# A two-layer hybrid encoder trunk: level masks made early on GpSimd, one product and one bank moved, and a stage's second chunk split between the halves of u

## The chip, the cores and the metric

The kernel runs as one program on one core of a Trainium2 chip. The core has TensorE (PE in the rows; PEld is its weight load), VectorE (DVE), ScalarE (ACT), GpSimd (POOL) and SyncE (SP), which run side by side and meet only at semaphores. The metric is the device time of one execution in microseconds (us), lower is better.

## The reference, cut to what matters

The input x is 512 tokens by 1024 channels, float32. Each of two layers does three residual stages:

```
x = x + 0.5 * rms_norm(swiglu(rms_norm(x), w_in, w_out))            # FFN, 2816 wide
u = rms_norm(x);  parts = u @ mix_w_in                              # mixer, 4872 wide
y_a = gated_delta_rule(conv+silu(q,k,v), beta, decay)  -> rms_norm * silu(z)
y_b = sliding_window_attention(rope(q), rope(k), v, sinks)
x = x + rms_norm((sig(gate_a) * (y_a @ w_a) + sig(gate_b) * (y_b @ w_b)) @ mix_w_out)
x = x + 0.5 * rms_norm(swiglu(...))                                 # second FFN
```

The delta rule works in chunks of 64 tokens. For each of 8 chunks and 4 heads it needs the inverse of a unit triangular 64x64 matrix A = I + lower(k_beta k^T * decay), the masked products q k^T * decay, and a state that is carried from chunk to chunk.

## The kernel before, in words

**Weights.** All weights come as one stream of chunks of 128x1024 float32. For each chunk SyncE loads `raw` (two slots), ScalarE rounds it to `whi` (L906, or L1243 for the first four chunks), and VectorE makes the remainder `wlo = raw - whi` (L1285). These two steps are called the split of a chunk. Both halves have a ring of four slots. SyncE may load chunk c+3 only when the split of chunk c+1 is done, since the slot of `raw` is free then. TensorE multiplies hi by hi, hi by lo and lo by hi (L520 to L522), 24 matmuls of 512 columns for a full chunk.

**Order of work.** Each engine has its own instruction list, written out by hand, and runs it strictly in order. In the mixer the lists come from one table, `mix_steps()`: for chunk j = 3 to 47 of the stage, after chunk j's matmuls (TensorE) or after the split of chunk j+3 (ScalarE, VectorE), each engine goes through the steps of `s[j]` and does its own part of each. A step that needs PSUM names its bank in `banks_of`. A bank goes from step to step in the order of the table: TensorE may fill it (`use`) only when the reader of the step before has given it back.

**The delta rule's inverse.** VectorE solves the 16x16 diagonal blocks by back substitution (step `solve`, s[14], L1539 and L1541, 30 small instructions that each wait for the one before). The blocks go out to DRAM and come back (SyncE, j = 16 and 17), and step `zb` (s[17]) spreads them to Z and its transpose Zt. Two levels (4 and 5) then join blocks of 16 to 32 and of 32 to 64. For each level and each half i of the 16 matrices: GpSimd multiplies the matrix by the level's mask into `Cs` (`level_mask`, L1738), TensorE multiplies Cs by Zt (`invp`, L719), ScalarE copies the result to `Pm` (L1122), which GpSimd has zeroed before (L1777), TensorE multiplies Pm by Z (`invd`, L731), and VectorE subtracts from Z and Zt (L1559). Level 4's masks are made by step `cmask` in s[14]. `Cs` and `Pm` exist once, so level 5's masks and zeroes are made in step `invp` of s[21], behind level 4's matmuls.

**Other steps of the change.** `vtr` transposes v (TensorE, then four ScalarE copies, L1116). `qtr` transposes q, and ScalarE squares it out of bank 5 (L1106) and gives the bank back (L1110). `qk` makes q k^T for 128 tokens (L705), and VectorE multiplies it into `attnT` (L1519). `sc` makes the attention scores in bank 5 (L783), VectorE finds their maximum (L1592 to L1595) and ScalarE takes the exponential (L1176) and gives the bank back. `evac` is ScalarE's copy of a finished PSUM tile to SBUF (L1050). Chunk 20 may write bank 0 only after `evac` 16 (tile `sk`), which stands in s[19].

**Between stages.** At a hand-over (`boundary`) the next stage's u is made while the last matmuls of the old stage run. u has two halves h of 256 tokens, each of eight pieces k. TensorE transposes the scaled x (`turn_tile`, L532) into the banks. For every k in turn ScalarE writes `uhi` (`u_round`, L956) and VectorE writes `ulo` (`u_rest`, L1327); piece k+2 of uhi waits for piece k of ulo. The first chunk of the new stage is split ahead of half 0, the second (c+1) behind it, then the third and fourth. TensorE's `first_group` begins with half 0: tiles m = 0 and 1 for k = 0 and 1, then tiles m = 2 and 3 for k = 0 and 1, then the second chunk. The transposes of half 0 lie in the same four banks as the tiles:

```
if h == 0 and k == 0:
    pe.wait_ge(u_lo.h, u_lo.at(L, u0 + (3, 4, 7, 8)[m]))
```

So tile 2 may start only when ulo piece 6 is written, and tile 3 when piece 7 is. There are five hand-overs with a next stage, and the same order stands once at the start of the kernel.

Of the kernel before, what the change touches and what calls it, by code (L numbers as in the profile page):

```python
# [79 lines left out]
def mix_steps():  # L80

    s = {j: [] for j in range(M_CHUNKS)}
    s[3] = [("evac", 0), ("evac", 1), ("ba",), ("evac", 2), ("evac", 3), ("conv", 0)]
    s[4] = [("bat",), ("gprep",), ("silu", 0), ("conv", 1)]
    s[5] = [("gsum",), ("conv", 2), ("silu", 1)]
    s[6] = [("conv", 3), ("silu", 2), ("decay", 0), ("decay", 1)]
    s[7] = [("evac", 4), ("evac", 5), ("evac", 6), ("evac", 7), ("silu", 3), ("off", 0), ("off", 1), ("conv", 4)]
    s[8] = [("ktr", 0), ("ktr", 1), ("conv", 5), ("silu", 4)]
    s[9] = [("ktr", 2), ("ktr", 3), ("knorm",), ("conv", 6), ("silu", 5)]
    s[10] = [("conv", 7), ("silu", 6), ("kk", 0), ("kk", 1)]  # L90
    s[11] = [("evac", 8), ("evac", 9), ("evac", 10), ("evac", 11), ("silu", 7), ("kk", 2), ("kk", 3), ("conv", 8)]
    s[12] = [("conv", 9), ("silu", 8)]
    s[13] = [("conv", 10), ("silu", 9)]
    s[14] = [("conv", 11), ("silu", 10), ("solve",), ("cmask",)]
    s[15] = [("evac", 12), ("evac", 13), ("evac", 14), ("evac", 15), ("silu", 11), ("swap", 0), ("swap", 1)]
    s[16] = [("vtr", 0), ("swap", 2), ("rope", 0), ("rope", 1)]
    s[17] = [("vtr", 1), ("swap", 3), ("zb",), ("vtr", 2)]
    s[18] = [("qk", 0), ("qk", 1), ("rope", 2), ("rope", 3)]
    s[19] = [("evac", 16), ("evac", 17), ("swap", 4), ("invp", 0, 4), ("vtr", 3), ("invp", 1, 4), ("rope", 4)]
    s[20] = [("vwin", 0), ("invd", 0, 4), ("qtr", 0), ("kmask",), ("invd", 1, 4)]  # L100
    s[21] = [("invp", 0, 5), ("vwin", 1), ("invp", 1, 5), ("qtr", 1), ("qk", 2), ("amask",)]
    s[22] = [("invd", 0, 5), ("invd", 1, 5), ("sc", 0)]
    s[23] = [("evac", i) for i in range(18, 22)] + [("zcp",), ("vx", 0), ("vx", 1)]
    s[22].insert(1, ("qtr", 2))
    s[23].insert(0, ("qtr", 3))
    s[24] = [("zx", 0), ("zx", 1), ("lq",)]
    s[25] = [("qk", 3)]
    s[26] = []
    for n in range(NCH):
        if n:  # L110
            s[22 + n].append(("sc", n))
        s[23 + n].insert(0, ("scn", n))
        s[24 + n].append(("pt", n))
        s[25 + n].append(("pv", n))
    for t in range(TT):
        if t:
            s[24 + 3 * t].append(("ks", t))
        s[25 + 3 * t].append(("sv", t))
        s[26 + 3 * t].append(("so", t))
        s[27 + 3 * t].append(("on", t))  # L120
        s[28 + 3 * t].insert(0, ("onm", t))
        s[29 + 3 * t].append(("otr", t))
    for i in range(4):
        s[24 + i].append(("zsilu", i))
    for g in range(4):
        s[27 + 4 * g] = [("evac", 22 + 4 * g + i) for i in range(4)] + s[27 + 4 * g]
    s[37] += [("ybs", 0), ("ybs", 1)]
# [13 lines left out]
def banks_of(step):  # L141

    k, x = step[0], (step[1] if len(step) > 1 else 0)
    if k in ("ba", "bat", "gsum", "vwin", "sc", "qtr"):
        return (5,)
    if k == "vtr":
        return ((5, 4, 6, 7)[x],)
# [64 lines left out]
def trunk(nc, wstream, xin, par, gpost, consts, rope, out):  # L212
# [3 lines left out]
    with ctx:  # L216
# [53 lines left out]
        Cs = at("Cs", [P, 16, CH], 52 * kb)  # L270
        Pm = at("Pm", [P, 16, CH], 56 * kb)
        tri = at("tri", [P, SB, SB], 57 * kb)
# [241 lines left out]
        def _(pe):  # L514
# [129 lines left out]
            def mixer(L):  # L644
# [6 lines left out]
                def do(step):  # L651
# [39 lines left out]
                    elif k == "qtr":  # L691
                        t = step[1]
                        use(L, step, 5)
                        pe.wait_ge(silu_done.h, silu_done.at(L, 12))
                        for h in range(H):
                            last = pe.transpose(bank(5, h * P, P), kq[:, 1, h, t * P:(t + 1) * P], ident)
                        done(last, 5)
                    elif k in ("kk", "qk"):
# [8 lines left out]
                    elif k == "invp":  # L707
# [9 lines left out]
                        for c in range(8 * i, 8 * i + 8):  # L717
                            for a in range(2):
                                last = pe.matmul(bank(b, (c % 8) * 32, 32, CH * a, CH * a + CH),  # L719
                                                 half(Cs, a, c), block_cols(half(Zt, a, c), lev, 0), start=True, stop=True)  # L720
                        done(last, b)
                    elif k == "invd":
                        i, lev = step[1], step[2]
                        got(("invp", i, lev), banks_of(("invp", i, lev))[0])
                        for n, b in enumerate(banks_of(step)):
# [175 lines left out]
        def _(act):  # L901
# [47 lines left out]

            def u_round(L, st, h):  # L950

                for k in range(KT):
                    act.wait_ge(turned.h, turned.at(L, 8 * (st - 1) + 4 * h + 3 + k // 4))
# [9 lines left out]
            def boundary(L, n, c, unit):  # L963
# [63 lines left out]
            def mixer(L):  # L1027
# [3 lines left out]
                def do(step):  # L1031
# [66 lines left out]
                    elif k == "qtr":  # L1098
                        t = step[1]
                        ready(step, 5)  # L1100
                        if t == 0:
# [3 lines left out]
                        for h in range(H):  # L1105
                            last = act.activation(tmp[:, 4 + t % 2, h * P:(h + 1) * P], bank(5, h * P, P), ACT.Square,  # L1106
                                                  accum_out=ssq[:, 4 * t + h:4 * t + h + 1])
                        last.then_inc(ssq_done.h, 1)
                        act.wait_ge(ssq_done.h, ssq_done.at(L, t + 1))
                        act.sem_inc(misc_out[5].h, 1)  # L1110
                    elif k == "vtr":
# [6 lines left out]
                    elif k == "invp":  # L1118
                        i, lev, b = step[1], step[2], banks_of(step)[0]
                        ready(step, b)  # L1120
                        act.wait_ge(p_zero.h, p_zero.at(L, 2 * (lev - LEVELS[0]) + i + 1))
                        act.activation(block_cols(Pm[:, 8 * i:8 * i + 8, :], lev, 0), half_cols(bank(b, 0, 256), lev),  # L1122
                                       ACT.Copy).then_inc(misc_out[b].h, 1)
# [126 lines left out]
            x_scale(0, 0, 1)  # L1250
            u_round(0, 0, 0)
            first_split(1)
            x_square(0, 0, 2)
            first_split(2)
# [14 lines left out]
        def _(dve):  # L1269
# [51 lines left out]

            def u_rest(L, st, h):

                for k in range(KT):
                    c = slice(2 * P * h, 2 * P * h + 2 * P)
# [4 lines left out]
            def boundary(L, n, c):  # L1330
# [352 lines left out]
            split(0, 0, 0)  # L1683
            u_rest(0, 0, 0)
            split(0, 1, 1)
            x_mean(0, 0, 2)
            split(0, 2, 2)
# [13 lines left out]
        def _(pool):  # L1701
# [32 lines left out]
            def mixer(L):  # L1734
                def level_mask(i, lev):

                    s8 = slice(8 * i, 8 * i + 8)
                    pool.tensor_tensor(Cs[:, s8, :], NN[:, s8, 0:CH], many(con[:, K_LEV + 64 * (lev - LEVELS[0]):][:, 0:64], 8),  # L1738
                                       ALU.mult).then_inc(c_done.h, 1)

                def do(step):
# [17 lines left out]
                    elif k == "cmask":  # L1759
                        pool.wait_ge(silu_done.h, silu_done.at(L, 11))  # L1760
                        for i in range(2):
                            level_mask(i, LEVELS[0])
                    elif k == "invp":
                        i, lev = step[1], step[2]
                        s8 = slice(8 * i, 8 * i + 8)
                        if lev == LEVELS[0]:
                            if i == 0:
                                pool.wait_ge(z1_done.h, z1_done.at(L, 2))
                        else:
                            last = ("invp", i, lev - 1)  # L1770
                            b = banks_of(last)[0]
                            pool.wait_ge(misc[b].h, misc[b].at(L, USE[last, b] + 1))
                            level_mask(i, lev)
                            used = ("invd", i, lev - 1)
                            pool.wait_ge(misc[banks_of(used)[0]].h, misc[banks_of(used)[0]].at(L, USE[used, banks_of(used)[0]] + 1))
                            pool.sem_inc(pool_begun.h, 1)
                        pool.memset(Pm[:, s8, :], 0.0).then_inc(p_zero.h, 1)  # L1777

# [156 lines left out]
```

## Time and profile before

| What | Value |
|---|---|
| Median of 3 runs | 2229.74 us (2229.63 to 2230.46) |
| The profiled execution's own time | 2229.16 us |
| Its span | 2227.4 us |
| TensorE busy | 2199.8 us of the span (99%), 11292 matmuls |
| VectorE, ScalarE, GpSimd busy | 1013.8, 841.5, 74.7 us (46%, 38%, 3%) |
| Mean granted TensorE clock | 0.999 of full speed |

A matmul's record is longer than the time to the next matmul's start, since matmuls are pipelined. Times of TensorE are therefore read from start to start: a 128x256 matmul follows the one before after 0.12 us, a 128x512 one after 0.23 us, and what is over that is a wait or a change of shape.

### The profile page before, as it was taken

The page shows a single profiled execution, that of the slowest core. Times are in us where ns is not written, and L with a number is a line of the kernel's source. Part 1 is how long each engine was busy: PE and PEld are TensorE (multiplying, and loading weights), DVE is VectorE, ACT ScalarE, POOL GpSimd, SP SyncE. Part 2 cuts the span into 40 slices and gives each one's busy share as a digit, 9 for nine tenths or more (in the row PEclk, how much of TensorE's full clock was granted, in tenths as well). Part 3 has the DMA queues.
Part 4 walks back from the last instruction along what each step waited for, and adds up shares of the span by engine and source line. Part 5 has one row for each costly group of instructions (what it writes and reads, how often), then busy time and mean ns, then how long its engine had stood idle before and what let it go on. Part 6 is the DMA issues. An engine that isn't in the chain of part 4 may idle for free. (4 is left out here: it accounts for less than half of the span.)

```text
span 2227.4 us, 28889 instructions
## 1 busy us (share of the span) xinstructions
PE 2199.8 (99%) x11292; PEld 1842.5 (83%) x11292; DVE 1013.8 (46%) x1438; ACT 841.5 (38%) x1491; POOL 74.7 (3%) x104
## 2 busy tenths in 40 slices
PE   7999999999999999999999999999999999999998
PEld 7888888888788888888888888887888888888887
DVE  4434324595536544342253433246954455344323
ACT  5323214656542533231252322156555425333211
POOL 0000000011000100000000000010100001000000
PEclk9999999999999999999999999999999999999999
DMA  4232222332223232223232232223322233322232
GB/s 164 95 101 93 99 95 83 126 84 76 67 76 139 90 111 95 94 94 104 78 113 95 94 104 94 95 76 133 83 68 67 85 142 97 103 95 94 96 102 77
DMA packets 71126, 215.83 MB, mean 97 GB/s; under 512 B 18928, under 2 KB 19440, under 8 KB 70256
## 3 DMA queue, kind: packets, MB, share of 16 engines
q1 hardware_dynamic: 69008, 201.82, 27.3%
q0 software_dynamic: 2016, 12.58, 1.6%
q8 instruction: 72, 1.18, 0.2%
q14 instruction: 30, 0.25, 0.0%
HBM read 206.77 MB, written 7.60 MB: 96 GB/s over the span
## 5 line engine op out<-in xcount | busy, mean ns | idle before, releaser
L1285 DVE TENSOR_TENSOR wlo<-raw,whi 128x1024 fp32r<-128x1024 f32 (+1 forms) x376 | 459.9, 1224 | 892.3 <-ACT whi L906 883.3
L520 PE MATMUL ps<-uhi,whi 128*128 128x512 f32 (+1 forms) x2208 | 826.8, 374 | 5.6 <-DVE ulo L1327 2.0
L522 PE MATMUL ps<-uhi,wlo 128*128 128x512 f32 (+1 forms) x2208 | 818.6, 371 | 0.0
L521 PE MATMUL ps<-ulo,whi 128*128 128x512 f32 (+1 forms) x2208 | 818.6, 371 | 0.0
L906 ACT ACTIVATE whi<-raw 128x1024 fp32r<-128x1024 f32 (+1 forms) x372 | 390.9, 1051 | 930.9 <-PE ps L522 549.0
L520 PEld LDWEIGHTS ps<-uhi,whi 128*128 128x128 f32 x2208 | 416.0, 188 | 80.0 <-issue 6.0
L522 PEld LDWEIGHTS ps<-uhi,wlo 128*128 128x128 f32 x2208 | 415.8, 188 | 71.7
L521 PEld LDWEIGHTS ps<-ulo,whi 128*128 128x128 f32 x2208 | 416.1, 188 | 69.4
L567 PE MATMUL ps<-whi,hhi 128*128 128x512 f32 x704 | 274.4, 390 | 0.0
L569 PE MATMUL ps<-whi,hlo 128*128 128x512 f32 x704 | 274.0, 389 | 0.0
L568 PE MATMUL ps<-wlo,hhi 128*128 128x512 f32 x704 | 273.9, 389 | 0.0
L569 PEld LDWEIGHTS ps<-whi,hlo 128*128 128x128 f32 x704 | 132.1, 188 | 27.7
L568 PEld LDWEIGHTS ps<-wlo,hhi 128*128 128x128 f32 x704 | 132.2, 188 | 27.2
L567 PEld LDWEIGHTS ps<-whi,hhi 128*128 128x128 f32 x704 | 132.2, 188 | 27.1
L993 ACT ACTIVATE tmp<-ps 128x512 f32<-128x512 f32 x88 | 52.8, 599 | 98.9 <-PE ps L522 98.5
L1366 DVE SCALAR_TENSOR_TENSOR tmp<-tmp,ps 128x512 f32<-128x512 f32 x88 | 60.2, 684 | 41.8 <-ACT tmp L993 41.8
L996 ACT ACTIVATE hhi<-tmp 128x512 f32 (+1 forms) x88 | 55.4, 629 | 52.1 <-DVE tmp L1369 52.1
L1710 POOL TENSOR_TENSOR ry<-msy,neghalf 128x1 f32<-128x1 f32 x24 | 17.9, 744 | 1492.9 <-DVE msy L1292 1492.9
L1375 DVE SCALAR_TENSOR_TENSOR hlo<-tmp,hhi 128x512 f32 (+1 forms) x88 | 60.6, 689 | 12.0 <-ACT hhi L996 10.8
L1369 DVE TENSOR_TENSOR tmp<-tmp,ps 128x512 f32<-128x512 f32 x88 | 60.5, 688 | 8.4 <-PE ps L522 1.2
L1469 DVE SCALAR_TENSOR_TENSOR tmp<-cv,prm,tmp 128x512 f32<-128x512 f32 x72 | 54.0, 750 | 8.1 <-ACT tmp L1057 6.4
L1327 DVE SCALAR_TENSOR_TENSOR ulo<-ps,prm,uhi 128x256 fp32r<-128x256 f32 x96 | 42.1, 480 | 28.9 <-ACT uhi L956 28.9
(213 smaller groups left out, 1548.2 us busy)
## 6 DMA issues: line engine op xcount, KB each, us to landing
raw<-in_wstream_dram SPq DMA_DIRECT2D x368, 512.0 KB, 3.4
x_home<-x POOLq DMA_DIRECT2D x4, 1024.0 KB, 4.4
x<-x_home POOLq DMA_DIRECT2D x2, 2048.0 KB, 8.5
gain<-in_gp_dram POOLq DMA_DIRECT2D x6, 512.0 KB, 6.2
x<-in_x_dram SPq DMA_DIRECT2D x4, 512.0 KB, 8.1
raw<-in_wstream_dram SPq DMA_DIRECT2D x8, 256.0 KB, 3.7
out_dram<-x SPq DMA_DIRECT2D x8, 256.0 KB, 2.0
rcs<-in_rope_dram POOLq DMA_DIRECT2D x2, 512.0 KB, 3.7
```

The source lines that it names most:

```text
L520: pe.matmul(o, lh, bhi, start=first, stop=False)
L521: pe.matmul(o, lh, blo, start=False, stop=False)
L522: return pe.matmul(o, ll, bhi, start=False, stop=last)
L567: pe.matmul(o, shi[:, k, tok], whi[:, s, w], start=k == 0, stop=False)
L568: pe.matmul(o, shi[:, k, tok], wlo[:, s, w], start=False, stop=False)
L569: last = pe.matmul(o, slo[:, k, tok], whi[:, s, w], start=False, stop=k == kn - 1)
L906: act.activation(whi[:, s, 0:cols], raw[:, s % RAWS, 0:cols], ACT.Copy).then_inc(hi_done.h, 1)
L996: act.activation(hhi[:, bass.ds(it * 2 + i, 1), :].rearrange("p a s -> p (a s)") if not isinstance(it, int) else hhi[:, 2 * it + i, :], tm ...
L1285: dve.tensor_tensor(wlo[:, s, 0:cols], raw[:, s % RAWS, 0:cols], whi[:, s, 0:cols].bitcast(f32), ALU.subtract) \
L1366: dve.scalar_tensor_tensor(tmp[:, i, :], tmp[:, 4 + i, :], 1.0, bank(4 * odd + 2 * i), ALU.add, ALU.mult).then_inc(tile_read.h, 1)
L1369: dve.tensor_tensor(tmp[:, 2 + i, :], tmp[:, i, :], bank(4 * odd + 2 * i + 1), ALU.mult).then_inc(tile_read.h, 1)
L1375: dve.scalar_tensor_tensor(lo, tmp[:, 2 + i, :], 0.5, hi.bitcast(f32), ALU.mult, ALU.subtract) \
```

## The change

Four edits:

1. In the mixer, `Cs` and `Pm` of level 5 get memory of their own (`Ctop`, `Ptop`; level 4's zeroed buffer becomes `Plow`). Step `cmask` (s[14]) now makes the masks of both levels, four GpSimd multiplications with two memsets between, and step `zb` zeroes level 5's buffer. Step `invp` has no GpSimd part any more.
2. `("vtr", 0)` goes from s[16] to s[19], behind the two evacs; `("qk", 3)` goes from s[25] to the end of s[31].
3. `("qtr", 3)` uses bank 4 instead of bank 5.
4. At every hand-over, and at the start of the kernel, the split of the second chunk goes from behind half 0 of u to between pieces 3 and 4 of it, on ScalarE and on VectorE. TensorE's order is as it was.

```diff
-    s[16] = [("vtr", 0), ("swap", 2), ("rope", 0), ("rope", 1)]
+    s[16] = [("swap", 2), ("rope", 0), ("rope", 1)]
-    s[19] = [("evac", 16), ("evac", 17), ("swap", 4), ("invp", 0, 4), ("vtr", 3), ("invp", 1, 4), ("rope", 4)]
+    s[19] = [("evac", 16), ("evac", 17), ("vtr", 0), ("invp", 0, 4), ("swap", 4), ("vtr", 3), ("invp", 1, 4), ("rope", 4)]
-    s[25] = [("qk", 3)]
+    s[25] = []
+    s[31] += [("qk", 3)]
-    if k in ("ba", "bat", "gsum", "vwin", "sc", "qtr"):
+    if k in ("ba", "bat", "gsum", "vwin", "sc"):
         return (5,)
+    if k == "qtr":
+        return ((5, 5, 5, 4)[x],)
...
-        Pm = at("Pm", [P, 16, CH], 56 * kb)
+        Cl = [Cs, at("Ctop", [P, 16, CH], 72 * kb)]
+        Pl = [at("Plow", [P, 16, CH], 76 * kb), at("Ptop", [P, 16, CH], 56 * kb)]
...
-            def u_round(L, st, h):
-                for k in range(KT):
+            def u_round(L, st, h, ks=range(KT)):
+                for k in ks:
...
-                u_round(L1, st, 0)
+                u_round(L1, st, 0, range(4))
                 next_split(L, c, 1, unit)
+                u_round(L1, st, 0, range(4, KT))
                 y_square(L, n, 3, unit)
...
-                u_rest(L1, st, 0)
+                u_rest(L1, st, 0, range(4))
                 split(L, c + 1, (c + 1) % RING)
+                u_rest(L1, st, 0, range(4, KT))
                 x_add(L, n, 2)
...
                         for i in range(2):
                             level_mask(i, LEVELS[0])
-                    elif k == "invp":
-                        ...
+                        for i in range(2):
+                            pool.memset(Pl[0][:, 8 * i:8 * i + 8, :], 0.0).then_inc(p_zero.h, 1)
+                        for i in range(2):
+                            level_mask(i, TOP)
+                    elif k == "zb":
+                        pool.wait_ge(z1_done.h, z1_done.at(L, 2))
+                        for i in range(2):
+                            pool.memset(Pl[1][:, 8 * i:8 * i + 8, :], 0.0).then_inc(p_zero.h, 1)
```

The start of the kernel has the same reordering around `first_split(1)` and `split(0, 1, 1)`.

## Rows read from the trace of the kernel before

**Rows 1.** The page, part 1: busy us, share of the span, instructions.

```profile
PE 2199.8 (99%) x11292; PEld 1842.5 (83%) x11292; DVE 1013.8 (46%) x1438; ACT 841.5 (38%) x1491; POOL 74.7 (3%) x104
```

**Rows 2.** Waits, whole span: engine, line, waited for: total us, times, longest.

```profile
PE ps L783 <- DVE attnT L1519: 2.6, 2, 1.3
PE ps L520 <- ACT sk L1050: 1.7, 2, 0.8
PE ps L783 <- ACTq L1110: 0.6, 2, 0.3
...
PEld ps L520 <- DVE wlo L1285: 3.2, 6, 0.5
...
PEld ps L532 <- ACT tmp L947: 2.5, 6, 0.5
```

**Rows 3.** Timeline, PE, first hand-over: start us, us, instruction, [idle before].

```profile
383.02 0.34 PE L520 MATMUL ps<-uhi,whi 128*128 128x256 f32 x1
...
384.39 0.28 PE L522 MATMUL ps<-uhi,wlo 128*128 128x256 f32 x1
384.99 0.38 PE L520 MATMUL ps<-uhi,whi 128*128 128x256 f32 x1 [0.32 <-DVE wlo L1285]
```

**Rows 4.** Timeline, ACT, the same hand-over.

```profile
379.69 0.87 ACT L956 ACTIVATE uhi<-ps,prm 128x256 fp32r<-128x256 f32 x2 [0.25 <-DVE ulo L1327]
...
382.63 1.05 ACT L906 ACTIVATE whi<-raw 128x1024 fp32r<-128x1024 f32 x1
```

**Rows 5.** Timeline, DVE, the same hand-over.

```profile
381.29 0.88 DVE L1327 SCALAR_TENSOR_TENSOR ulo<-ps,prm,uhi 128x256 fp32r<-128x256 f32 x2 [0.21 <-ACT uhi L956]
382.37 0.88 DVE L1327 SCALAR_TENSOR_TENSOR ulo<-ps,prm,uhi 128x256 fp32r<-128x256 f32 x2 [0.21 <-ACT uhi L956]
383.71 1.23 DVE L1285 TENSOR_TENSOR wlo<-raw,whi 128x1024 fp32r<-128x1024 f32 x1 [0.46 <-ACT whi L906]
```

**Rows 6.** Timeline, ACT, the fourth chunk's split in that hand-over.

```profile
388.40 1.06 ACT L906 ACTIVATE whi<-raw 128x1024 fp32r<-128x1024 f32 x1 [0.95 <-DMA raw<-in_wstream_dram]
```

**Rows 7.** Timeline, PE, start of the kernel.

```profile
18.50 0.36 PE L520 MATMUL ps<-uhi,whi 128*128 128x256 f32 x1 [0.51 <-DVE ulo L1327]
```

**Rows 8.** Timeline, POOL, layer 0: masks and memsets.

```profile
483.89 2.54 POOL L1738 TENSOR_TENSOR Cs<-NN,con 128x512 f32<-128x512 f32 x2 [26.91 <-DVE kq L1482]
...
512.46 0.53 POOL L1777 MEMSET Pm<- 128x512 f32 x1 [8.36 <-PE ps L731]
```

**Rows 9.** Timeline, DVE, layer 0: the substitution and what follows it.

```profile
483.94 1.29 DVE L1541 TENSOR_TENSOR sol<-sol,prod 128x15 f32<-128x15 f32 x1
485.26 1.22 DVE L1539 TENSOR_TENSOR prod<-tri,sol 128x28 f32<-128x28 f32 x1
486.51 0.19 DVE L1541 TENSOR_TENSOR sol<-sol,prod 128x28 f32<-128x28 f32 x1
...
492.97 0.69 DVE L1285 TENSOR_TENSOR wlo<-raw,whi 128x512 fp32r<-128x512 f32 x1
...
498.67 1.23 DVE L1285 TENSOR_TENSOR wlo<-raw,whi 128x1024 fp32r<-128x1024 f32 x1
...
512.74 0.69 DVE L1587 TENSOR_TENSOR tmp<-tmp 128x512 f32<-128x512 f32 x1
```

**Rows 10.** Timeline, ACT, layer 0, before chunk 20.

```profile
503.39 1.06 ACT L906 ACTIVATE whi<-raw 128x1024 fp32r<-128x1024 f32 x1 [0.30 <-DMA raw<-in_wstream_dram]
504.35 0.58 ACT L1050 ACTIVATE sk<-ps 128x512 f32<-128x512 f32 x1
```

**Rows 11.** Timeline, PE, layer 0: chunk 20 begins.

```profile
505.08 0.47 PE L520 MATMUL ps<-uhi,whi 128*128 128x512 f32 x1 [0.81 <-ACT sk L1050]
```

**Rows 12.** Timeline, PE, layer 0: qk 3, and the scores behind it.

```profile
556.11 1.05 PE L705 MATMUL ps<-kq 128*128 128x128 f32 x8
...
559.67 0.67 PE L783 MATMUL ps<-skz,sq 128*128 128x256 f32 x2 [1.33 <-DVE attnT L1519]
```

**Rows 13.** Timeline, ACT, layer 0: last read of the scores before.

```profile
554.97 0.21 ACT L1176 ACTIVATION_READ_ACCUMULATOR pexp<-ps,mneg 128x1 f32 x1
```

More of the change, by code:

```diff
@@ L691, in do @@
                     elif k == "qtr":
-                        t = step[1]
-                        use(L, step, 5)
+                        t, b = step[1], banks_of(step)[0]
+                        use(L, step, b)
                         pe.wait_ge(silu_done.h, silu_done.at(L, 12))
                         for h in range(H):
-                            last = pe.transpose(bank(5, h * P, P), kq[:, 1, h, t * P:(t + 1) * P], ident)
-                        done(last, 5)
+                            last = pe.transpose(bank(b, h * P, P), kq[:, 1, h, t * P:(t + 1) * P], ident)
+                        done(last, b)
                     elif k in ("kk", "qk"):
@@ L719, in do @@
                                 last = pe.matmul(bank(b, (c % 8) * 32, 32, CH * a, CH * a + CH),
-                                                 half(Cs, a, c), block_cols(half(Zt, a, c), lev, 0), start=True, stop=True)
+                                                 half(Cl[lev - LEVELS[0]], a, c), block_cols(half(Zt, a, c), lev, 0), start=True, stop=True)
                         done(last, b)
@@ L723, in do @@
                         i, lev = step[1], step[2]
+                        Pm = Pl[lev - LEVELS[0]]
                         got(("invp", i, lev), banks_of(("invp", i, lev))[0])
@@ L1098, in do @@
                     elif k == "qtr":
-                        t = step[1]
-                        ready(step, 5)
+                        t, b = step[1], banks_of(step)[0]
+                        ready(step, b)
                         if t == 0:
@@ L1105, in do @@
                         for h in range(H):
-                            last = act.activation(tmp[:, 4 + t % 2, h * P:(h + 1) * P], bank(5, h * P, P), ACT.Square,
+                            last = act.activation(tmp[:, 4 + t % 2, h * P:(h + 1) * P], bank(b, h * P, P), ACT.Square,
                                                   accum_out=ssq[:, 4 * t + h:4 * t + h + 1])
@@ L1109, in do @@
                         act.wait_ge(ssq_done.h, ssq_done.at(L, t + 1))
-                        act.sem_inc(misc_out[5].h, 1)
+                        act.sem_inc(misc_out[b].h, 1)
                     elif k == "vtr":
@@ L1121, in do @@
                         act.wait_ge(p_zero.h, p_zero.at(L, 2 * (lev - LEVELS[0]) + i + 1))
-                        act.activation(block_cols(Pm[:, 8 * i:8 * i + 8, :], lev, 0), half_cols(bank(b, 0, 256), lev),
+                        act.activation(block_cols(Pl[lev - LEVELS[0]][:, 8 * i:8 * i + 8, :], lev, 0), half_cols(bank(b, 0, 256), lev),
                                        ACT.Copy).then_inc(misc_out[b].h, 1)
@@ L1250, in _ @@
             x_scale(0, 0, 1)
-            u_round(0, 0, 0)
+            u_round(0, 0, 0, range(4))
             first_split(1)
+            u_round(0, 0, 0, range(4, KT))
             x_square(0, 0, 2)
@@ L1320, in x_mean, with u_rest @@
                 dve.tensor_scalar(msx[:, t:t + 1], ssx[:, t:t + 1], 1.0 / D, EPS, ALU.mult, ALU.add).then_inc(msx_done.h, 1)
-            def u_rest(L, st, h):
-                for k in range(KT):
+            def u_rest(L, st, h, ks=range(KT)):
+                for k in ks:
                     c = slice(2 * P * h, 2 * P * h + 2 * P)
@@ L1683, in _ @@
             split(0, 0, 0)
-            u_rest(0, 0, 0)
+            u_rest(0, 0, 0, range(4))
             split(0, 1, 1)
+            u_rest(0, 0, 0, range(4, KT))
             x_mean(0, 0, 2)
@@ L1737, in level_mask @@
                     s8 = slice(8 * i, 8 * i + 8)
-                    pool.tensor_tensor(Cs[:, s8, :], NN[:, s8, 0:CH], many(con[:, K_LEV + 64 * (lev - LEVELS[0]):][:, 0:64], 8),
+                    pool.tensor_tensor(Cl[lev - LEVELS[0]][:, s8, :], NN[:, s8, 0:CH], many(con[:, K_LEV + 64 * (lev - LEVELS[0]):][:, 0:64], 8),
                                        ALU.mult).then_inc(c_done.h, 1)
@@ L1762, in do @@
                             level_mask(i, LEVELS[0])
-                    elif k == "invp":
[L1764 to L1777, printed above, removed]
+                        for i in range(2):
[6 more added lines that the diff above has]
+                            pool.memset(Pl[1][:, 8 * i:8 * i + 8, :], 0.0).then_inc(p_zero.h, 1)
                 pool.wait_ge(u_lo.h, u_lo.at(L, 16))
```

## The prediction

> **What bounds the kernel now.** I read the page's busy shares first: TensorE is busy 99% of the span and no other engine half of it [rows 1]. A busy share of 99% leaves 27.6 us (2227.4 - 2199.8) in which TensorE has nothing, and since none of the four edits adds or removes a matmul, only these gaps can move. The second view is the list of waits, cut to TensorE and its weight load [rows 2]. Here the reader is to see how small and how placed the gaps are. The scores (L783) wait twice for qk 3's multiplication on VectorE (1.3 us each), chunk 20 waits twice for the `sk` copy, the scores wait twice for qtr 3's bank, the second chunk of a stage waits six times for `wlo`, and the transposes of a hand-over wait for the scaled x (six times, at most 0.5 each; one is at the start of the kernel, so some 2.0 over the five hand-overs). All that the change aims at is therefore about 10 us. The third view is the timeline of each engine around each of these places, since a fix of 0.5 us is easily paid for with an instruction of 1.2 us in front of something else.
>
> **Edit 4, the second chunk between the pieces of u.** Now TensorE ends the first chunk's half with a matmul at 384.39 and starts the second chunk at 384.99 [rows 3]. At a pitch of 0.12 that is 0.48 too late, and about 0.1 more goes in the restart: 0.6 per place. It waits for the `wlo` of 383.71 + 1.23 = 384.94 [rows 5]. But the same rows show what stood ahead of it: tile 2 started at 383.02, on the very tick at which ulo piece 6 allowed it (the pair of pieces 6 and 7 starts at 382.37). There is no slack on that second wait.
>
> With the new order: uhi pieces 2 and 3 end at 379.69 + 0.87 = 380.56. `whi` takes 1.05 and overlaps the end of the pair ahead a little [rows 4]: it ends near 381.50. `wlo` follows 0.03 later and takes 1.23: 382.76. The four remaining ulo pieces come in two pairs, 1.09 apart (381.29, 382.37) [rows 5]; the first can start at 382.68, the last at 383.77 instead of 382.37, 1.40 later. Tile 2 then starts at about 384.40 instead of 383.02. Twelve matmuls follow before the second chunk, which has its split at 382.76 and waits no more. So 1.38 is lost and 0.6 is won: +0.8 per place. ScalarE could hide its share (its 1.05 us runs while VectorE works), VectorE could not: its split is in series with ulo.
>
> Something comes back later in the hand-over. The split of c+1 ends 2.2 us earlier (382.76 for 384.94), so SyncE's load of the fourth chunk starts 2.2 earlier, and ScalarE's wait of 0.95 for it goes [rows 6]. The scaled x of tokens 384 to 511 stands behind it on ScalarE and comes between 0 and 0.95 earlier, while TensorE arrives 0.8 later. So the wait of at most 0.5 in each of five places [rows 2] goes wholly. At the start of the kernel the third tile already waits 0.51 for ulo [rows 7]; there the same insertion costs the same 0.8 and there is nothing to win back. Sum of edit 4: 6 x 0.8 - 2.0 = +2.8 us. Bounds: if ulo 6 and 7 were not delayed, 6 x -0.6 - 2.0 = -5.6; if nothing comes back, 6 x 0.8 = +4.8, and a full 1.38 at six places without the won 0.6 is +8.3.
>
> **Edit 1, all masks in the substitution.** Level 4's two masks are made there already, 2.54 us for two [rows 8]. Within just these 2.54 us the two VectorE instructions that run take 1.29 and 1.22 us, and the first after them, of the same kind, takes 0.19 [rows 9]. Each has two SBUF inputs and stood still until GpSimd's multiplication was over. The two masks thus cost VectorE (1.29 - 0.19) + (1.22 - 0.19) = 2.1 us. Two more masks in the same chain cost the same again: +2.1 per layer. The masks that go from s[20] and s[21] blocked whole-chunk splits there; nothing on TensorE's side waited for these, so their removal is priced at 0.
>
> The two memsets: a memset at 512.46 to 512.99 overlaps a two-input VectorE instruction at 512.74, which takes its usual 0.69 [rows 8, 9]. I take 0 for them. Upper end: 0.53 each, 1.06 per layer.
>
> The Trainium skill has a rule on this, SBUF — State Buffer, section "Who interferes with whom": a VectorE instruction with two SBUF inputs contends with a GpSimd instruction that reads SBUF and not with one that only writes it, and the later one to issue blocks fully. The page's section "Terms" says more broadly that the shared pair is exclusive for the full instruction, which taken alone would charge the memsets too. By the first the sum is mine, by the second it is the rival with the memsets below. The memset row speaks for the first.
>
> Is the substitution on TensorE's path? VectorE runs without an idle row from the substitution over the split of chunk 18 (492.97) to the split of chunk 20 (498.67, ends 499.90) [rows 9]. That last one lets SyncE load chunk 22, whose `whi` ScalarE starts at 503.39 after waiting for that DMA, then the `sk` copy at 504.35 to 504.93, then chunk 20 at 505.08 with 0.81 idle [rows 9 to 11]. Every link is tight, so all of 2.1 arrives at chunk 20, whatever part of it TensorE has waited for at chunk 18 before. That TensorE has 0.6 us less in s[16] and as much more in s[19] (vtr 0) changes only where it waits: the copy of `sk`, near 507.0, stays the last to come. Net +2.1 per layer. Lower bound 0 (the delay is absorbed in a slack that I do not see), upper 2 x 1.28 + 1.06 = 3.6.
>
> **Edit 2, qk 3 out of s[25].** TensorE's 8 matmuls move, nothing is saved by that. Scores 3 start at 559.67 after 1.33 idle [rows 12]; where the second chunk waited, the start came 0.16 later than the idle says (0.48 against 0.32, rows 3), so 1.5 us are lost here. Bank 5 must wait for qk 3's multiplication, which VectorE reaches late. Without it bank 5 is held by scores 2, whose last read ends at 554.97 + 0.21 = 555.18 [rows 13], while TensorE arrives near 559.67 - 1.5 - 0.9 = 557.3 (0.9 for the eight matmuls that are gone, 1.05 with the last one's tail). Slack 2 us, so no new wait: -1.5 per layer. In s[31] qk 3 costs what it cost, and its reader needs it only in s[35]. Bounds -1.6 and 0.
>
> **Edit 3, qtr 3 in bank 4.** The scores' wait of 0.3 [rows 2] goes. Next late is the copy of tile 18 on ScalarE, which stands behind the same squares and which chunk 24 needs; it leaves about half: -0.15 per layer, bounds -0.4 and 0.
>
> **Sum.** +2.8 + 2 x (2.1 - 1.5 - 0.15) = +3.7 us. Against the profiled execution's own 2229.16 that gives 2232.9; the median of the runs shown is 0.6 above that execution, so the forecast is 2233.5, 0.17% more than before. What a measurement of this kernel can tell from no change is about 0.2%, or 4.5 us: the forecast is a small loss inside that.
>
> **Rivals.**
>
> A, slower: the shared SBUF access charges GpSimd's whole time in the substitution, memsets too, in series with the chain above: 3.6 instead of 2.1 per layer, +3.0, 2236.5. For it: tight chain, and four GpSimd instructions in a row leave no gap. Against it: the memset row. It decides from 2.5 us per layer upwards, where the total passes 4.5.
>
> B, no change: the new masks don't reach TensorE (VectorE's small instructions slip between them, or chunk 20 was late for another reason): -2 x 2.1, 2229.3. Against it: two blocked instructions out of two.
>
> C, faster: the split between the pieces does not delay tiles 2 and 3, because VectorE finishes it while it would idle for uhi. Then edit 4 gives its -5.6 instead of +2.8: 2225.1. For it: VectorE idles 0.21 per pair [rows 5]. Against it: these are 0.42 of the 1.23 that the split takes.
>
> **Chances.** The forecast 0.62, of which about a third lies past 4.5 us, since its own range is 2231.5 to 2235.5; A 0.15; B 0.14; C 0.09. Faster by over 0.2% (below 2225.3): 0.08; slower (above 2234.2): 0.35; within: 0.57. The range takes in B's middle and A's: 2229.3 to 2236.8.
>
> **What would show it.** Right: TensorE's list of waits has `ulo` instead of `wlo` at the six first groups, near 1.2 us each, and no wait of L532 for `tmp`; four VectorE instructions of the substitution are over 1 us instead of two, and chunk 18 waits about 2 us for its split; L783 waits no more for L1519 or L1110; the fourth chunk's `whi` no longer waits for its DMA. Wrong: a first group without a wait for `ulo` (then C), a substitution of 9.1 us as now (483.9 to 493.0, rows 8 and 9; then B), one of over 12.3 us (then A), or scores 3 still idle, for ScalarE's scores 2 or VectorE's softmax.

## The result

Before takes 2229.91 us (median of 9 runs, 2229.14 to 2232.23) and after 2236.55 us (9 runs, 2234.43 to 2238.49). The ratio is 1.0028, with a 95% interval of 1.0019 to 1.0036: the change makes the kernel slower by about 6.6 us, or 0.28%, which is small and clear of the interval. The profiled execution of after took 2236.55 us, with a span of 2234.8; the span before was 2227.4, so 7.4 us are to be found between the two traces.

The page of after, part 1 (busy us, share of the span, instructions), beside [rows 1]:

```profile
PE 2204.0 (99%) x11292; PEld 1846.8 (83%) x11292; DVE 1013.1 (45%) x1438; ACT 840.4 (38%) x1491; POOL 71.8 (3%) x104
```

TensorE executes the same 11292 matmuls, yet it is *busy* for 4.2 us longer (2204.0 against 2199.8). Only 3.2 of the 7.4 us are idle time. A wait makes an engine hardly busier (in [rows 3] the record behind a wait is 0.38 long, the one ahead of it 0.28), so this line already says that something besides the waits has changed.

The list of TensorE's waits of after (engine, line, waited for: total us, times, longest), all of it without its weight load, beside [rows 2]:

```profile
PE ps L536 <- ACT tmp L952: 10.9, 1, 10.9
PE ps L524 <- DVE ulo L1334: 8.1, 7, 1.4
PE ps L524 <- DVE wlo L1292: 4.7, 2, 2.4
PE ps L524 <- ACT sk L1056: 0.6, 1, 0.6
```

The line on `ulo` has this one in its place in the kernel before, both of its waits at the start of the kernel:

```profile
PE ps L520 <- DVE ulo L1327: 2.0, 2, 1.5
```

The first line of after is the start of the kernel. The scores' line (L788 here) is gone from the list, both for `attnT` and for the bank, and so are the scaled-x waits of the five hand-overs. New are five waits of 1.2 for `ulo`, in the place of those for `wlo` at a stage's start, and 2.4 and 2.3 us for `wlo` at chunk 18 of the two layers.

The first hand-over, timeline of TensorE (start us, us, instruction, [idle before]), beside [rows 3]:

```profile
385.22 0.35 PE L524 MATMUL ps<-uhi,whi 128*128 128x256 f32 x1 [1.20 <-DVE ulo L1334]
...
386.72 0.28 PE L524 MATMUL ps<-uhi,whi 128*128 128x256 f32 x1
```

Tile 2 starts 2.20 later than in [rows 3] (385.22 for 383.02), of which 0.82 was there already, from the start of the kernel: 1.38 are new. The second chunk (386.72) has no bracket, so no wait, and is 1.73 later (384.99 before): 0.47 is won back. VectorE and ScalarE in that hand-over, beside [rows 4 to 6]:

```profile
382.37 1.23 DVE L1292 TENSOR_TENSOR wlo<-raw,whi 128x1024 fp32r<-128x1024 f32 x1 [0.46 <-ACT whi L911]
383.51 0.87 DVE L1334 SCALAR_TENSOR_TENSOR ulo<-ps,prm,uhi 128x256 fp32r<-128x256 f32 x2
384.59 0.88 DVE L1334 SCALAR_TENSOR_TENSOR ulo<-ps,prm,uhi 128x256 fp32r<-128x256 f32 x2 [0.21 <-ACT uhi L961]
```

```profile
387.88 1.04 ACT L911 ACTIVATE whi<-raw 128x1024 fp32r<-128x1024 f32 x1
```

The split stands between the two halves of `ulo`, for 1.23 us in series. The fourth chunk's `whi` starts without the 0.95 of waiting for its DMA [rows 6].

The substitution in layer 0, VectorE, beside [rows 9]:

```profile
485.35 1.29 DVE L1549 TENSOR_TENSOR sol<-sol,prod 128x15 f32<-128x15 f32 x1
486.68 1.22 DVE L1547 TENSOR_TENSOR prod<-tri,sol 128x28 f32<-128x28 f32 x1
487.94 0.19 DVE L1549 TENSOR_TENSOR sol<-sol,prod 128x28 f32<-128x28 f32 x1
...
488.87 1.25 DVE L1549 TENSOR_TENSOR sol<-sol,prod 128x48 f32<-128x48 f32 x1
490.16 1.22 DVE L1547 TENSOR_TENSOR prod<-tri,sol 128x55 f32<-128x55 f32 x1
...
496.44 0.69 DVE L1292 TENSOR_TENSOR wlo<-raw,whi 128x512 fp32r<-128x512 f32 x1
```

GpSimd beside it, for [rows 8]:

```profile
485.31 2.55 POOL L1747 TENSOR_TENSOR Cs<-NN,con 128x512 f32<-128x512 f32 x2 [26.95 <-DVE kq L1490]
487.80 0.99 POOL L1773 MEMSET Plow<- 128x512 f32 x2
488.75 2.55 POOL L1747 TENSOR_TENSOR Ctop<-NN,con 128x512 f32<-128x512 f32 x2
```

Four VectorE instructions of over 1.2 us (all four are shown), two within each pair of multiplications; within the memsets (487.80 to 488.79) the one shown takes its usual 0.19. The way from the first blocked instruction to the split of chunk 18 is 11.1 us long (485.35 to 496.44), where it was 9.0 [rows 9].

And what follows on TensorE, with the granted clock. First the timeline at chunk 18 and at 541, then stretches of the span (window: length, busy time and count of PE, PEld, DVE, ACT, POOL; granted clock; DMA share; GB/s):

```profile
497.18 0.79 PE L524 MATMUL ps<-uhi,whi 128*128 128x512 f32 x1 [2.41 <-DVE wlo L1292]
...
540.75 0.63 PE L525 MATMUL ps<-ulo,whi 128*128 128x512 f32 x1
541.18 0.51 PE L526 MATMUL ps<-uhi,wlo 128*128 128x512 f32 x1
541.53 0.39 PE L524 MATMUL ps<-uhi,whi 128*128 128x512 f32 x1
541.75 0.39 PE L525 MATMUL ps<-ulo,whi 128*128 128x512 f32 x1
```

```profile
494.00:497.00 3.00, 0.77 (x8) 0.53 (x5) 2.66 (x12) 0.16 (x1) 0.00 (x0) 1.00 0.01 3
497.00:500.30 3.30, 3.12 (x7) 2.48 (x8) 3.27 (x7) 0.00 (x0) 0.00 (x0) 0.51 0.69 206
...
531.00:537.80 6.80, 6.80 (x110) 5.89 (x109) 2.35 (x4) 1.14 (x8) 0.00 (x0) 1.00 0.25 77
537.90:541.20 3.30, 3.30 (x14) 2.77 (x13) 1.66 (x6) 0.86 (x6) 0.95 (x1) 0.52 0.02 5
...
1643.80:1647.10 3.30, 3.30 (x15) 2.85 (x14) 1.66 (x6) 0.71 (x6) 0.95 (x1) 0.52 0.02 5
```

The clock column is the one to read. It stands at 0.51 to 0.52 (0.50, which is 1.2 GHz, with the start of each window just ahead of it) in three stretches of 3.4 us; from 50 us to the last matmul the rest is at 1.00 (2.4 GHz), as in the lines ahead of two of them. Both kernels also end at half clock, for some 4 us behind their last matmul, where it costs nothing. The timeline shows what that does to one matmul of 512 columns: 0.43 us from start to start at 540.75, 0.22 at 541.53, where the clock is back. In the kernel before the clock is 1.00 in the stretches with the same work:

```profile
494.50:498.00 3.50, 3.50 (x23) 3.12 (x22) 3.46 (x6) 0.43 (x1) 0.00 (x0) 1.00 0.89 192
...
534.00:537.00 3.00, 3.00 (x16) 2.54 (x16) 1.90 (x6) 0.97 (x7) 0.96 (x1) 1.00 0.02 5
```

The whole difference can be booked by setting each matmul's start in one trace against the same matmul's in the other, and noting where the distance between them steps. In us: start of the kernel and five hand-overs +2.84; way to chunk 20 +2.92 in layer 0 and +1.97 in layer 1; scores 1 -0.20 and -0.23; scores 3 -2.45 and -2.43 at the old place of qk 3, and +0.88 and +0.93 later at its new one; the half-clock stretches near 538 and 1644 +1.59 and +1.56. The sum is 7.4, as is the difference of the spans. Layer 0's way to chunk 20 is 0.95 longer than layer 1's, which has the same stall and the full clock behind it; this I put to the stretch at 497. (That stretch takes 1.5 us like the others, but part of it falls into time that TensorE waited for `sk` before: that wait is left in layer 1 alone.) The clock thus took 0.95 + 1.59 + 1.56 = 4.1 us, and the forecast's terms make the other 3.3.

For the first matmuls of the kernel the clock column is no guide: it reads 1.00 there in every trace. In after the first twelve matmuls of 128x256 stand 0.21 apart (from 16.35 us), in before 0.12, which is near the ratio of the two clocks. In after this costs nothing: TensorE waits for `ulo` behind them in any case, and the step at the start is 0.82 here and 0.79 in the trace of experiment 7, where these matmuls stand 0.12 apart. It does add to the busy time: experiment 6, slow in this way at its start and with no fall later, is busy for 2200.8 us.

### The profile page after: what moved, and what is told of

Its sections match the earlier page's. It is cut to its first block and busy times, and to the rows that moved or that the text cites. A ratio compares the mean times of both kernels' runs of the same rounds, so it can differ in the third digit from the quotient of the medians.

```text
span 2234.8 us, 28885 instructions
## 1 busy us (share of the span) xinstructions
PE 2204.0 (99%) x11292; PEld 1846.8 (83%) x11292; DVE 1013.1 (45%) x1438; ACT 840.4 (38%) x1491; POOL 71.8 (3%) x104
```

## The experiments

Each ran 11 times, interleaved with the kernel before on the same chip. They ran in three groups, each on a chip of its own, so times of different groups are compared through the kernel before of the same group. The first four separate the parts of the change.

**1. The u split alone**, added to the kernel before (ScalarE's side; VectorE's has the same cut around its split of c + 1).

```
-                u_round(L1, st, 0)
+                u_round(L1, st, 0, range(4))
                 next_split(L, c, 1, unit)
+                u_round(L1, st, 0, range(4, KT))
```

> The kernel before with edit 4 alone (second chunk split between the pieces of u, at the five hand-overs and at the start). My theory, the pieces 6 and 7 of ulo come late: TensorE waits for ulo ahead of tile 2 for 1.2 to 1.4 us in six places, no longer for wlo, and no longer for the scaled x; 2.8 us slower. Rival, all of edit 4's terms were a matter of the mixer's later start: no change. Rival, the granted clock falls as in the kernel after: 1.5 us more per fall.

Measured: 2234.22 us (2231.24 to 2237.28) against 2230.06; ratio 1.0016 (1.0007 to 1.0026). The first of its new waits on TensorE:

```profile
PE ps L520 <- DVE ulo L1329: 8.1, 7, 1.4
```

The `ulo` line is the same as in after, 8.1 us in seven waits, and each hand-over steps by +1.36 to +1.37 at tile 2 and back by 0.45 to 0.47 at the second chunk. In the trace, with no fall of the clock, the steps from the first matmul on sum to +2.9 (the first matmul itself is 0.9 earlier than in before, so the spans differ by 2.0 only). So edit 4 alone is a loss and rival C (faster by 5.6) falls. The median is 1.3 us above what the steps give; where is not shown, as its one trace is of its fastest run. Three of its 11 runs have a mean granted clock of 0.998, which none of the 33 runs of before beside it has, so a share of the clock is likely.

**2. qk 3 to s[31] and qtr 3 to bank 4, alone.**

```
-    s[25] = [("qk", 3)]
+    s[25] = []
...
+    s[31] += [("qk", 3)]
...
+    if k == "qtr":
+        return ((5, 5, 5, 4)[x],)
```

> The kernel before with edits 2 and 3 alone but for vtr 0 (qk 3 at the end of s[31], qtr 3 in bank 4). My theory: scores 3 wait for nothing, 1.5 us per layer, and 0.15 per layer at scores 1: 3.3 us faster. Rival: in the kernel after the gain was only so large since VectorE's chain stood differently; here VectorE's softmax takes the place of the wait and it gains under 1 us.

Measured: 2227.91 us (2225.53 to 2230.84) against 2230.06; ratio 0.9989 (0.9980 to 0.9998). The steps of its trace sum to -3.2 from the first matmul on (spans -2.8, with 0.4 at the start), and scores 3 start without a wait; in the timeline of TensorE at 557:

```profile
557.66 1.03 PE L786 MATMUL ps<-skz,sq 128*128 128x256 f32 x4
```

Beside [rows 12], the 1.33 us of waiting has gone and nothing took its place, so the rival (a gain under 1 us) falls. These two edits are a gain: 3.2 by the trace, 2.1 by the medians. That trace is of one of its faster runs (2226.39), and the difference of 1.1 is not explained.

**3. The masks alone** (with vtr 0's move, which belongs to the order that they need).

```
                         for i in range(2):
                             level_mask(i, LEVELS[0])
+                            pool.memset(Pl[0][:, 8 * i:8 * i + 8, :], 0.0).then_inc(p_zero.h, 1)
...
+                        for i in range(2):
+                            level_mask(i, TOP)
```

> The kernel before with edit 1 and vtr 0's move alone. My theory: two more blocked instructions of 1.2 us in each substitution, chunk 18 waits 2.4 us, 2.1 us per layer at chunk 20: 4.2 us slower with the clock full, and 1.0 to 1.5 us more for each stretch of half clock. Rival, the clock does most of it: where the trace shows no fall the loss is under 2 us.

Measured: 2235.53 us (2234.51 to 2237.87) against 2230.06; ratio 1.0024 (1.0015 to 1.0033). That is 5.5 us, where the blocked instructions explain 4.2 (2.1 per layer). Windows of it, behind the stall of layer 0, then in and behind that of layer 1:

```profile
496.00:500.00 4.00, 2.24 (x10) 1.86 (x11) 3.83 (x11) 0.00 (x0) 0.00 (x0) 1.00 0.42 126
...
1600.00:1603.00 3.00, 0.72 (x8) 0.48 (x6) 2.68 (x12) 0.06 (x1) 0.00 (x0) 1.00 0.00 0
1603.20:1606.40 3.20, 3.20 (x8) 2.47 (x8) 3.17 (x6) 0.00 (x0) 0.00 (x0) 0.50 0.89 222
```

Here the clock falls behind layer 1's stall and not behind layer 0's (first line, 1.00); in after it was the other way round. The same wait is followed by the fall in one place and not in the other. From the first matmul on, this trace (of the slowest run) is 8.0 us longer than that of before: 2.1 on the way to chunk 20 in layer 0, at full clock, 2.9 in layer 1, 1.6 for a second half-clock stretch at 1644, and 1.2 in the first 50 us, where the code is that of before but the matmuls of 128x256 stand 0.21 apart until 22.4 us. The 2.1 at full clock is what answers the rival, which gave the clock most of the loss.

By the ratios the parts of experiments 1, 2 and 3 add up to the whole: +0.16 - 0.11 + 0.24 = +0.29%, and after is at +0.28%.

**4. After without the u split.**

```
-                u_round(L1, st, 0, range(4))
+                u_round(L1, st, 0)
                 next_split(L, c, 1, unit)
-                u_round(L1, st, 0, range(4, KT))
```

> The kernel after with edit 4 undone. My theory: 2.9 us faster than the kernel after, so about 3.7 us slower than before, of which 0.9 is masks less qk 3 and bank, the rest stretches of half clock. Rival, the falls of the clock come from edit 4: then none is left here and it is 0.9 us slower than before.

Measured: 2231.79 us (2229.82 to 2235.53) against 2230.06; ratio 1.0010 (1.0001 to 1.0019). After stands at 1.0028, so taking edit 4 away gives back about 4.0 us, within the intervals the same as the 4.2 of experiment 1. Its windows at the stall of layer 0:

```profile
493.00:496.60 3.60, 1.10 (x9) 0.81 (x8) 3.24 (x13) 0.08 (x1) 0.00 (x0) 1.00 0.06 19
496.70:500.00 3.30, 3.30 (x10) 2.53 (x9) 3.27 (x7) 0.00 (x0) 0.00 (x0) 0.50 0.95 205
```

The fall at 497 is here too, those of 538 and 1644 are not. The loss of 1.7 us lies between the 3.7 that was expected and the rival's 0.9. The steps of this trace give the same 1.7 from the first matmul on, with 3.1 on the way to chunk 20 in layer 0 and, at full clock, 2.1 in layer 1. Other runs of this kernel lost more to the clock than its trace shows: two have a mean clock of 0.996 (2234.82 and 2235.53) and two of 0.997, against 0.999 in the profiled one. So edit 4 is not what brings the falls, or not alone.

The next two ask whether GpSimd's reading or its mere running blocks VectorE. Both add two GpSimd instructions to the kernel before, right behind level 4's masks, into memory that nothing reads.

**5. Two more multiplications.**

```
+                        for i in range(2):
+                            s8 = slice(8 * i, 8 * i + 8)
+                            pool.tensor_tensor(spare[:, s8, :], NN[:, s8, 0:CH], many(con[:, K_LEV + 64:][:, 0:64], 8), ALU.mult)
```

> The kernel before with two more GpSimd multiplications of 128x512 in the substitution, behind the two that are there, into memory that nothing reads. My theory, reads of SBUF by GpSimd stop VectorE's two-input instructions: two more instructions of the substitution take about 1.2 us, chunk 18 waits about 2 us, 4.2 us slower in all. Rival, memory or order of the moved steps did it: no change here.

Measured: 2234.66 us (2233.21 to 2236.09) against 2230.38; ratio 1.0018 (1.0009 to 1.0027). The added instructions on GpSimd, and VectorE beside them:

```profile
487.18 2.58 POOL L1767 TENSOR_TENSOR spare<-NN,con 128x512 f32<-128x512 f32 x2
```

```profile
487.29 1.23 DVE L1543 TENSOR_TENSOR sol<-sol,prod 128x28 f32<-128x28 f32 x1
488.56 1.25 DVE L1541 TENSOR_TENSOR prod<-tri,sol 128x39 f32<-128x39 f32 x1
489.85 0.20 DVE L1543 TENSOR_TENSOR sol<-sol,prod 128x39 f32<-128x39 f32 x1
```

The two shown first are blocked by the added multiplications, as two others are by the old ones; the next is at 0.20. The two added multiplications reach TensorE, with no other part of the change in place: +4.3 us by the medians, so 2.1 per layer. The trace itself shows more, 3.0 and 2.5 on the way to chunk 20, because the clock falls behind the stall of chunk 18 in both layers:

```profile
496.80:500.00 3.20, 3.20 (x8) 2.55 (x9) 3.17 (x6) 0.00 (x0) 0.00 (x0) 0.50 0.80 223
1602.70:1605.90 3.20, 3.20 (x9) 2.53 (x8) 3.17 (x6) 0.04 (x1) 0.00 (x0) 0.50 0.91 200
```

Its mean clock is 0.998 (2234.78), while eight of the eleven runs have 0.999 or 1.000.

**6. Two memsets of twice the columns.**

```
+                        for i in range(2):
+                            pool.memset(spare2[:, 1024 * i:1024 * i + 1024], 0.0)
```

> The kernel before with two GpSimd memsets of 1024 columns (1.0 us each) in the same place. My theory, writes alone stop nothing: every instruction of the substitution but the two known ones stays under 0.25 us, no change of the time. Rival, any GpSimd instruction holds VectorE: 2.0 us more per substitution, 3.5 to 4 us slower.

Measured: 2230.51 us (2229.39 to 2231.76) against 2230.38; ratio 0.9999 (0.9990 to 1.0008). GpSimd, and VectorE beside it:

```profile
486.57 1.86 POOL L1766 MEMSET spare<- 128x1024 f32 x2
```

```profile
486.72 0.19 DVE L1543 TENSOR_TENSOR sol<-sol,prod 128x28 f32<-128x28 f32 x1
```

GpSimd is busy for 1.86 us and VectorE runs through it undisturbed. Rival A falls: the memsets cost nothing. Both runs agree with the Trainium skill, SBUF — State Buffer, section "Who interferes with whom": a GpSimd instruction that reads SBUF contends with a two-input VectorE instruction, one that only writes does not.

**7. After, with TensorE kept at work in the stall.** Ten matmuls of 512 columns whose results nothing uses, ahead of chunk 18 in each layer.

```
+                    if j == 18:
+                        use(L, ("vtr", 0), 5)
+                        for i in range(10):
+                            pe.matmul(bank(5, 0, SEQ, 0, 16), bab[:, 0:16], uhi[:, i % KT, :], start=True, stop=True)
```

> The kernel after with ten matmuls of 512 columns (2.3 us, results unused) on TensorE between chunk 17 and the wait of chunk 18, so that it works where it stood still. If the idle stretch makes the clock fall at 497 us: that fall is gone, and the time is some 0.8 to 1.5 us below the kernel after; the falls near 540 and 1645 us may stay. Rival, the fall has nothing to do with the idle stretch: same clock and same time, or slower by what the filler is too long.

Measured: 2233.65 us (2233.0 to 2236.58) against 2230.38; ratio 1.0014 (1.0005 to 1.0023), where after has 1.0028 (1.0019 to 1.0036). By the ratios that is about 3 us less for twenty more matmuls; the two intervals still overlap. Timeline of TensorE, then windows behind it:

```profile
495.23 2.55 PE L862 MATMUL ps<-uhi,bab 128*16 128x512 f32 x10
497.93 0.50 PE L524 MATMUL ps<-uhi,whi 128*128 128x512 f32 x1 [0.16 <-DVE wlo L1296]
```

```profile
497.90:501.30 3.40, 3.37 (x17) 2.87 (x18) 3.37 (x6) 0.00 (x0) 0.00 (x0) 1.00 0.77 214
...
537.90:541.20 3.30, 3.30 (x12) 2.82 (x11) 1.67 (x6) 0.99 (x8) 0.95 (x1) 0.50 0.02 5
```

Chunk 18 starts as late as it must, for its split is as late, but the stretch behind it is at 1.00, and so is that of layer 1. The falls near 538 and 1644 stay. This trace is of the kernel's slowest run (2236.58), so it shows more than the median pays. By its steps the filled stall is worth 0.8 us: the way to chunk 20 is +2.1 in both layers, where after has +2.9 and +2.0. That is the size that was expected. The other 2 us of the difference in the medians is not in this trace; the runs' mean clocks say that most of them also lack the falls near 538 and 1644 (nine of eleven runs have 0.999 or 1.000, in after two of nine), and why the filler should do that is not shown.

**8. Another way to take the `wlo` wait away.** The second chunk's split stays behind the whole of half 0 of u, but is made in two halves of 512 columns, and TensorE starts on the first.

```
-                split(L, c + 1, (c + 1) % RING)
+                halves_lo(L1, st, c + 1 - (L1 - L) * LAYER_CHUNKS, (c + 1) % RING)
...
+            def halves_lo(L, st, c, s):
+
+                for i, (hi, done, at_) in enumerate(((mid_hi, mid_done, st + 1), (hi_done, split_done, c + 1))):
+                    w = slice(SEQ * i, SEQ * i + SEQ)
+                    dve.wait_ge(hi.h, hi.at(L, at_))
+                    dve.tensor_tensor(wlo[:, s, w], raw[:, s % RAWS, w], whi[:, s, w].bitcast(f32), ALU.subtract).then_inc(done.h, 1)
```

> The kernel before with the second chunk of a stage split in two halves of 512 columns behind half 0 of u, TensorE starting on the first half when that is there (one more instruction each on ScalarE and VectorE, 0.1 us). My theory: the wlo wait of 0.6 us goes in six places, nothing else moves: 3.3 us faster. Rival: the extra instruction delays x_add and so the transposes of the last tokens, and half of it is given back: 1.5 us faster.

Measured: 2228.93 us (2226.18 to 2230.53) against 2230.38; ratio 0.9992 (0.9983 to 1.0001). From its timelines and its waits:

```profile
383.35 1.29 DVE L1306 TENSOR_TENSOR wlo<-raw,whi 128x512 fp32r<-128x512 f32 x2
```

```profile
384.57 0.28 PE L521 MATMUL ps<-uhi,whi 128*128 128x256 f32 x1
```

```profile
PEld ps L533 <- ACT tmp L952: 3.6, 6, 0.7
```

The 0.6 of each place is won and tile 2 is not delayed. Part of it is given back at the next thing that is late, the scaled x: 3.6 us in six waits, where it was 2.5 [rows 2]. Another 0.5 goes on the way to chunk 20 in the two layers, of which experiments 2 and 6 show 0.3 to 0.4 too, without a part of the change in that place. From the first matmul on the trace is 1.8 us shorter. By time alone the gain is not certain, as the interval reaches 1.

**9. The gains together**: the kernel before with the edits of experiments 2 and 8, and without the masks and the u split.

> The kernel before with qk 3 at the end of s[31], qtr 3 in bank 4, and the second chunk in halves behind half 0 of u; no mask moved. My theory, the terms add: 2.1 us for qk 3 and bank and 1.5 us for the halves as measured alone (3.3 us each by the traces): 3.6 to 6 us faster than before, 2224 to 2227 us. Rival, the halves give their part back at the transposes of the last tokens: 2 us faster.

Measured: **2225.25 us** (2223.89 to 2226.73) against 2229.97; ratio 0.9978 (0.9969 to 0.9987). It is 4.7 us faster than before, as expected, and some 11 faster than after. Two of its waits on TensorE:

```profile
PE ps L536 <- ACT tmp L955: 13.3, 6, 11.4
PE ps L524 <- ACT sk L1065: 1.6, 2, 0.9
```

The largest part of the first is the start of the kernel (11.4); the 1.9 left are the five hand-overs' waits for the scaled x. No wait for `attnT` or at tile 2 is in the list.

Its one trace also has a half-clock stretch near 1634, with no idle time ahead of it:

```profile
1628.00:1634.10 6.10, 6.10 (x107) 5.31 (x107) 1.61 (x3) 1.14 (x8) 0.00 (x0) 1.00 0.26 86
1634.30:1637.50 3.20, 3.20 (x11) 2.72 (x11) 1.66 (x6) 0.91 (x7) 0.95 (x1) 0.50 0.02 5
```

## Why the prediction was right, and where it was short

The forecast was 2233.5 us, a small loss; it came to 2236.55, a loss of 6.6 instead of 3.7. The stated range (2229.3 to 2236.8) holds, but the forecast's own (2231.5 to 2235.5) does not: the range reaches so far because it takes in rival A, which gives 2236.5. What rival A describes did not happen, so that the time lies in the range is in part luck. The forecast also put the loss inside of what can be told from no change (0.57 for that, 0.35 for a clear loss), and it came out clear.

**Edit 4: right in size.** Forecast +2.8, in the trace of after +2.8, alone +2.9. Each step came as worked out: tile 2 was to be 1.38 later and is; 0.6 was to be won at the second chunk and 0.58 is (0.47 at its start, the rest in the restart); 2.0 was to come back at the scaled x and 2.0 does, by steps of 0.3 to 0.5. The wait for `ulo` is 1.2 in the five hand-overs and 0.66 at the start of the kernel, where it was expected to be near 1.2 too. The rule behind it: an order that is already tight on VectorE (tile 2 started on the tick of its `ulo`) can't take a 1.2 us instruction in front of it to save 0.6 behind it.

**Edit 1: right in what blocks and in what it costs.** Four blocked instructions; 2.1 forecast per layer, 2.0 found at full clock in after and 2.1 in experiments 3 and 4. Experiment 5 shows the same alone, 6 that reading is what counts. Rival B (masks don't reach TensorE) falls with 5. Rival A falls with 6 and with the length of the substitution, 11.1 us where A asked for over 12.3.

**Edits 2 and 3: right.** -1.5 forecast, -1.57 and -1.50 found; -0.15 forecast, -0.20 and -0.23 found.

**What was missing: a term for the clock.** The sum charged every wait its own length and took TensorE's clock as given, as the trace of before shows no half-clock stretch where the change works. In the profiled execution of after there are three, and they cost 4.1 us. The forecast's own terms come to 3.3 us in that trace, for 3.7. That the medians are only 6.6 apart, and the two traces 7.4, is the profiled execution of before, which was 0.75 faster than its median. The nine runs of after agree in part: the two with a mean granted clock of 0.999 took 2234.43 and 2234.95 us, within 1.5 of the forecast, the two with 0.996 took 2237.77 and 2238.49. But the two with 0.998 (2236.61 and 2237.66) lie above the three with 0.997 (2235.83 to 2236.55), so the clock is not all that differs from run to run.

**What brings the falls.** In the traces, a stall of 1.8 to 2.5 us at chunk 18 with TensorE idle comes eight times (after and experiments 3, 4 and 5, two layers each), and the clock falls behind five of them. In the twelve places where chunk 18 waits for less than 0.2 us (before and experiments 1, 2, 6, 8 and 9) it never falls, nor behind the two that experiment 7 fills. The mean clocks of all runs point the same way. A mean of 0.998 or less have 26 of the 42 runs with the long stall, 2 of 11 with the stall filled, 6 of the 55 of experiments 1, 2, 6, 8 and 9, and 2 of the 81 runs of before beside them. So the longer stall makes falls more frequent. It is not a fixed price: in after layer 1's stall passed without one. What decides in a single execution is open, and two filled stalls in one trace would not show by themselves that the filling removed the fall.

The stretches near 538 and 1644 stay open. They follow the products of level 5 (107 to 110 matmuls in 6.1 to 6.8 us, most of them small) with no idle time ahead, and appear in the traces of after, experiments 3 (1644 alone), 7 and, near 1634, 9, but not in the traces of before, 1, 2, 4, 5, 6 and 8, which have the same products. No experiment here changed the products themselves, and each kernel has one trace, so I can't say what decides. I don't claim them for the edits: part of the 2.9 us by which the loss exceeds the forecast may be the luck of how the work falls in time.

That edit 4 costs 4.0 to 4.2 us by medians (experiments 1 and 4) and 2.9 by its trace is open for the same reason; a share of the clock's is likely, and not shown.

## What to carry to other kernels

Before an instruction is put ahead of another to cure a wait of 0.6 us, look whether what it displaces starts on the tick of its own input; if so, its whole duration is the price, and halving the instruction behind it (experiment 8) cures the wait without that price, though that gain is not certain by time alone. GpSimd work that reads SBUF beside a chain of short VectorE instructions costs that chain one full GpSimd instruction each time (1.2 to 1.3 us here, experiment 5), and memsets, which only write, cost it nothing (experiment 6). In a kernel whose TensorE is 99% busy, compare busy time, not only waits: where the same matmuls are busy for several us more (2204.0 against 2199.8 here), look at the granted clock. A wait of 2.4 us can cost another 0.9 behind it.

## What the runs showed of the hardware that was not expected

- The granted clock fell to 1.2 GHz for 3.4 us directly behind a stall of 1.8 to 2.5 us in a TensorE that was otherwise fully busy (after at 497, experiment 3 at 1603, experiment 4 at 497, experiment 5 in both layers), and in three other places the same stall left it at 2.4 GHz.
- It also fell with no stall at all, behind 6 to 7 us of TensorE 100% busy with over a hundred matmuls, most of them small (after at 538, experiment 9 at 1634), at a price of about 1.6 us each time.
- Ten 512-column matmuls into 16 rows, results unused, take 2.55 us within the stall, and in the one trace the stretch behind them stays at 2.4 GHz in both layers (experiment 7).
- The first matmuls of 128x256 of an execution stand 0.21 or 0.12 us apart: 0.21 in after and experiments 1, 3, 6 and 9, 0.12 in before and experiments 2, 4, 5, 7 and 8, though the code of the start is the same in before and in experiments 2 to 6. It cost 1.2 us in experiment 3, where it lasted until 22.4 us, and some 0.5 in experiment 9 (the step at the start is -0.07 there and -0.58 in experiment 8), and nothing in after and in experiment 6.
